# Product keys: gathering the rows of the picked experts instead of streaming all of U and V

## The reference

```python
def _peer(h, w_q, sub_keys, u_tab, v_tab):
    q = (xt @ w_q).reshape(n, PEER_HEADS, 2, PEER_QDIM // 2)
    s = jnp.einsum('nhpd,phkd->nhpk', q, sub_keys).astype(jnp.float32)
    s1, i1 = lax.top_k(s[:, :, 0], K)
    s2, i2 = lax.top_k(s[:, :, 1], K)
    comb = (s1[..., :, None] + s2[..., None, :]).reshape(n, PEER_HEADS, K * K)
    cand = (i1[..., :, None] * PEER_NKEYS + i2[..., None, :]).reshape(n, PEER_HEADS, K * K)
    top_s, pos = lax.top_k(comb, K)
    experts = jnp.take_along_axis(cand, pos, axis=-1)
    gate = jax.nn.softmax(top_s, axis=-1).astype(h.dtype)
    ...
        a = jax.nn.gelu(jnp.einsum('nd,nhkd->nhk', xc, u_tab[ec]))
        return jnp.einsum('nhk,nhkd->nd', gc * a, v_tab[ec])
```

## Time and profile before

| | us |
|---|---|
| median of 3 runs | 2853.23 (2847.7 to 2858.61) |
| span of the profiled execution | 2849.9 |
| TensorE busy | 2686.8 |
| VectorE busy | 1420.1 |
| ScalarE busy | 1154.0 |
| POOL busy | 73.7 |
| DMA moved | 784.12 MB |

### The profile page before, as it was taken

How to read it: one execution, slowest core, us unless ns; L and a number is a source line. 1 busy time by engine, 2 the same in 40 slices (tenths; PEclk the granted TensorE clock), 3 DMA queues, 4 the chain that set the end, 5 groups by cost and what they waited for, 6 DMA issues and landing times.

```text
span 2849.9 us, 53267 instructions
## 1 busy us (share of the span) xinstructions
PE 2686.8 (94%) x20480; PEld 2122.4 (74%) x20480; DVE 1420.1 (50%) x2985; ACT 1154.0 (40%) x2104; POOL 73.7 (3%) x140
## 2 busy tenths in 40 slices
PE   6989989999999999998999999999999999989997
PEld 5769955554545555554878999999998888788997
DVE  2545532222221222222356658887657777656783
ACT  3344321221112211221244454467775544555772
POOL 0000000000000000000000000000000100000000
PEclk9999989999999999999999999999999999999999
DMA  6765689999999989999475556655547777623452
GB/s 246 273 260 220 240 329 422 422 422 422 421 422 423 422 360 422 422 422 393 152 297 203 188 181 222 219 187 168 181 166 251 243 240 241 219 107 131 158 187 104
DMA packets 113215, 784.12 MB, mean 275 GB/s; under 512 B 13488, under 2 KB 13488, under 8 KB 21936
## 3 DMA queue, kind: packets, MB, share of 16 engines
q1 hardware_dynamic: 101808, 741.39, 67.1%
q0 software_dynamic: 11264, 40.71, 4.1%
HBM read 763.96 MB, written 18.09 MB: 274 GB/s over the span
## 4 chain that ended last, share of the span: by engine, by line
PE 78%; DMA 12%; DVE 3%; ACT 3%; SPq 2%; issue 2%; POOL 0%; DVEq 0%; ACTq 0%; POOLq 0%
PE psum L804 15%; PE psum L1451 12%; PE psum L1417 12%; PE psum L1084 11%; DMA weight_ring<-in_stream 9%; PE psum L1116 5%; PE psum L1543 2%; PE psum L671 2%; DMA work<-in_stream 2%; SPq L1599 2%; PE psum L1037 2%; PE psum L1436 2%; PE psum L1046 2%; PE psum L823 1%; PE psum L731 1%
## 5 line engine op out<-in xcount | busy, mean ns | idle before, releaser
L2046 DVE TENSOR_TENSOR work<-psum,work 128x256 f32<-128x256 f32 x132 | 56.1, 425 | 690.6 <-PE psum L1057 690.6
L1678 DVE TENSOR_TENSOR ring_parts<-weight_ring,peer_parts 128x1024 fp32r<-128x1024 f32 x218 | 262.3, 1223 | 252.8 <-ACT peer_parts L2749 208.9
L2749 ACT ACTIVATE peer_parts<-weight_ring 128x1024 fp32r<-128x1024 f32 x218 | 225.0, 1054 | 264.9 <-PE psum L804 118.7
L1116 PE MATMUL psum<-work 128*64 128x512 f32 x1056 | 244.9, 600 | 25.9 <-ACT work L2917 19.3
L1084 PE MATMUL psum<-weight_ring,work 128*64 128x256 f32 x2112 | 244.9, 382 | 16.6 <-DMA weight_ring<-in_stream 15.7
L1451 PE MATMUL psum<-v_high,h_low 128*128 128x512 f32 x1024 | 254.6, 391 | 2.9 <-ACT v_high L3111 2.9
L1084 PEld LDWEIGHTS psum<-weight_ring,work 128*64 128x64 f32 x2112 | 146.5, 137 | 116.0 <-DMA weight_ring<-in_stream 34.1
L1451 PEld LDWEIGHTS psum<-v_high,h_low 128*128 128x128 f32 x1024 | 193.1, 189 | 43.2 <-issue 3.0
L2385 DVE TENSOR_TENSOR ring_parts<-weight_ring,peer_parts 128x1024 fp32r<-128x1024 f32 x128 | 156.8, 1225 | 101.4 <-ACT peer_parts L3067 101.1
L3111 ACT ACTIVATE v_high<-weight_ring 128x1024 fp32r<-128x1024 f32 x128 | 135.8, 1061 | 171.4 <-PE psum L1451 171.4
L2899 ACT ACTIVATE work<-psum 128x256 f32<-128x256 f32 x132 | 50.7, 384 | 363.4 <-PE psum L1084 363.4
(11 more groups left out here) (348 smaller groups left out, 4532.2 us busy)
## 6 DMA issues: line engine op xcount, KB each, us to landing
weight_ring<-in_stream SPq DMA_DIRECT2D x451, 1024.0 KB, 5.3
work<-in_stream SPq DMA_DIRECT2D x192, 1024.0 KB, 23.7
chunkbuf<-in_stream SPq DMA_DIRECT2D x64, 1024.0 KB, 23.6
peer_scores<-chunkbuf POOLq DMA_DIRECT2D x61, 256.0 KB, 5.4
chunkbuf<-peer_scores POOLq DMA_DIRECT2D x61, 256.0 KB, 2.9
work<-in_rows POOLq DMA_DIRECT2D x1, 1312.0 KB, 16.8
xT<-in_x POOLq DMA_DIRECT2D x1, 1024.0 KB, 10.2
work<-in_ctx POOLq DMA_DIRECT2D x1, 1024.0 KB, 18.7
```

The costliest lines, as they stand in the source:

```text
L1116: mm = pe.matmul(psum[h * SEATS:(h + 1) * SEATS, 7, :], m["act_e"][:, 2 * k + f, :], w[:, f, h * 512:(h + 1) * 512], start=(k == 0 and f = ...
L1678: ve.tensor_tensor(split[s].at(ring_parts, q), split[s].at(ring, q), high_halves[:, q % HIGHS, :].bitcast(F32), ALU.subtract).then_inc(spl ...
L2749: sc.activation(high_halves[:, q % HIGHS, :], split[s].at(ring, q), ACT.Copy).then_inc(split[s].high, 1)
```

## The change

The tables U and V lie side by side in one HBM tensor `in_uv` of 16,384 rows of 2048 floats (8 KB), with tokens on the partitions for this layer. A unit is one head of one half of the tokens: 16 units of 16 picks, 256 picks g. For each:

- POOL gathers, for the 128 tokens of its half, the row `expert[token, g]` of `in_uv` into one of 8 places (`EARLY`), 11 from g = 64 on (`LATE` = 3, which lie where the queries and keys were). It waits until the value product of the pick that held the place before is done.
- VectorE multiplies the U half of the row by h (`h_nat`, turned once by TensorE) and sums along the row (`scored`).
- ScalarE takes the gelu of that one number a token, multiplies it by the gate, and writes the identity scaled by it, a diagonal (`diagonal`).
- TensorE multiplies the diagonal by the V half of the row, in plain fp32, 2 x 512 columns, and adds it in PSUM (`values_of`).

The search for unit u+2 stands between the 16 products of unit u on VectorE. The queries and keys of heads 4 to 7 stand between value products on TensorE. `keys` is no longer a piece of the ring but is loaded by POOL. The round trips of x and of the scores, G, the one-hot tables and the 128 streamed pieces are gone, and the result of the first half of the tokens is turned and added to x while the second half is worked on. Weight halves of stage 3 that stood at the layer's end (`highs(0)`, `lows(0)`, `highs(1)`, `lows(1)`) stand between the last picks.

```diff
+EARLY, LATE = 8, 3
+DIAGS = 4
...
-    ("peer_q", 8), ("keys", 1), ("peer", PE_N),
+    ("peer_q", 8),
...
+                def values_of(g):
+                    t = g // (PICKS // TT)
+                    pe.wait_ge(pick_d, g + 1)
+                    for h in range(2):
+                        mm = pe.matmul(psum[:, 2 * t + h, :], m["diag"][:, g % DIAGS, :],
+                                       m["rows_of_uv"][row_place[g]][:, D + h * 512:D + (h + 1) * 512],
+                                       start=(g % (PICKS // TT) == 0), stop=True, skip_group_check=True)
+                    mm.then_inc(pick_v, 1)
...
+                for g in range(PICKS):
+                    if g in (8, 20, 32, 44):
+                        queries(4 + g // 12)
+                    if g in (10, 22, 34, 46):
+                        keyed(4 + g // 12, 5 + 2 * (g // 12 % 2))
...
+                    values_of(g)
...
+                def scored(g):
+                    t, row = g // (PICKS // TT), m["rows_of_uv"][row_place[g]][:, 0:D]
+                    ve.wait_ge(*row_landed(g))
+                    ve.tensor_tensor_reduce(row, row, m["h_nat"][:, t, :], 1.0, 0.0, ALU.mult, ALU.add,
+                                            m["score"][:, g:g + 1]).then_inc(pick_s, 1)
...
+                searched(0, weights_beside)
+                searched(1, lambda k: None)
+                gated(0)
+                gated(1)
...
+                def diagonal(g):
+                    one = slice(g, g + 1)
+                    sc.wait_ge(pick_s, g + 1)
+                    sc.activation(m["gelu"][:, one], m["score"][:, one], ACT.Gelu_apprx_tanh).then_inc(pick_a, 1)
+                    if g % PE_K == 0:
+                        sc.wait_ge(*at(f"gate:{g // PE_K}"))
+                    sc.wait_ge(pick_a, g + 1)
+                    sc.activation(m["weight"][:, one], m["gelu"][:, one], ACT.Copy, scale=m["gate"][:, one]).then_inc(pick_c, 1)
+                    if g >= DIAGS:
+                        sc.wait_ge(pick_v, g - DIAGS + 1)
+                    sc.wait_ge(pick_c, g + 1)
+                    sc.activation(m["diag"][:, g % DIAGS, :], ident[:, :], ACT.Copy, scale=m["weight"][:, one]).then_inc(pick_d, 1)
...
+                for g in range(PICKS):
+                    before = row_before(g)
+                    if g % PE_K == 0:
+                        gp.wait_ge(*at(f"expert:{g // PE_K}"))
+                    if before is not None:
+                        gp.wait_ge(pick_v, before + 1)
...
+                    gp.indirect_dma_start(m["rows_of_uv"][row_place[g]], None, dram["uv"],
+                                          bass.IndirectOffsetOnAxis(ap=m["expert"][:, g:g + 1], axis=0)) \
+                      .then_inc(row_in[row_place[g]], 16)
...
-    u = np.concatenate([u[0::2], u[1::2]], 2)
...
+    W["uv"] = np.concatenate([a["peer_u_2"][0], a["peer_v_2"][0]], 1)
```

More of the change, by code:

```diff
@@ L590, in plan @@
-                m["zs"] = a.take(2, PE_H)
-                m["G"] = work[:, :].rearrange("p (t k) -> p t k", t=T)
-                tables = xT[:, :, :].rearrange("p c t -> p (c t)").rearrange("p (q s k n) -> p q s k n", q=2, s=2, k=CHUNK)
-                last = work[:, 32768 - 2 * CHUNK * PE_N:32768].rearrange("p (q k n) -> p q k n", q=2, k=CHUNK)
-                m["oh1"], m["oh2"] = ([tables[:, q, 0], tables[:, q, 1], last[:, q]] for q in range(2))
-                whole = chunkbuf[:, :, :].rearrange("p a b -> p (a b)")
@@ new lines, in plan @@
+                late = [a.at]
+                m["h_low"] = as_parts(a.take(DC, T), a.at - DC * T)
+                m["sc"] = a.take(TT, 16, PE_N)
+                late.append(a.at)
+                m["pqT"] = a.take(8, T)
+                m["diag"] = a.take(DIAGS, P)
+                m["expert"] = a.take(PICKS).bitcast(U32)
+                m["sums"], m["shares"] = a.take(UNITS), a.take(UNITS)
+                rows_at = 32768 - (EARLY - 1) * SLOT
+                assert a.at <= rows_at
+                late.append(32768 - SLOT)
@@ L2587, in mix3 @@
+                for u in range(UNITS):
+                    unit(u)
+                    if u == PE_H:
+                        residual_of_picks(0, V, mod_cols(2, 5))
+                ve.wait_ge(pick_v, PICKS)
+                ve.tensor_copy(m["y_nat"][:, 1, 512:D], psum[:, 3, :]).then_inc(*V.up("free:y:1:1", "y_nat:1:1"))
+                residual_of_picks(1, V, mod_cols(2, 5))
             def mix3():
@@ L3138, in peer, with exponentials_of_picks @@
[L3138 to L3141 removed]
+                def exponentials_of_picks(u):
+                    sc.wait_ge(*at(f"cand:{u}"))
+                    gate = m["gate"][:, u * PE_K:(u + 1) * PE_K]
+                    act(A_, gate, gate, ACT.Exp, f"cand_exp:{u}", accum_out=m["sums"][:, u:u + 1])
@@ new lines, in peer @@
+                queries(0)
+                queries(1)
+                highs(26, 2)
+                for i in range(4):
+                    sc.wait_ge(*at(f"h_nat:{i}"))
+                    act(A_, m["h_nat"][:, i // 2, (i % 2) * 512:(i % 2 + 1) * 512], bank_of(f"h_nat:{i}"), ACT.Copy,
+                        f"free:h_nat:{i}", *(["h_nat_sb"] if i == 3 else []))
+                scores_of_keys(0)
+                scores_of_keys(1)
+                highs(27, 2)
+                queries(2)
+                scores_of_keys(2)
@@ new lines, in peer @@
+                highs(28, 2)
+                queries(3)
+                scores_of_keys(3)
+                exponentials_of_picks(0)
+                exponentials_of_picks(1)
+                for g in range(PICKS):
+                    diagonal(g)
+                    if g in (9, 21, 33, 45):
+                        queries(4 + g // 12)
+                    if g in (11, 23, 35, 47):
+                        scores_of_keys(4 + g // 12)
+                    if g in (10, 11, 22, 23, 34, 35):
+                        high_half(58 + 2 * (g // 12) + g % 12 - 10, 2)
+                    if g % PE_K == 13 and g // PE_K + 2 < UNITS:
+                        exponentials_of_picks(g // PE_K + 2)
+                    if g == PICKS // TT + 3:
+                        sc.wait_ge(pick_v, PICKS // TT)
+                        for h in range(2):
+                            act(A_, m["y_nat"][:, 0, h * 512:(h + 1) * 512], psum[:, h, :], ACT.Copy, f"free:y:0:{h}",
+                                f"y_nat:0:{h}")
+                    if g in (234, 236, 238, 240):
+                        high_half((g - 234) // 2)
```

608 lines of the change are left out of this document (190 added, 418 removed).

## The result

| | before | changed |
|---|---|---|
| median, us | 2855.92 (2847.7 to 2858.99, 4 runs) | 2696.43 (2693.96 to 2698.39, 4 runs) |
| span of the profiled execution | 2849.9 | 2696.2 |
| TensorE busy | 2686.8 | 2412.8 |
| VectorE busy | 1420.1 | 1243.5 |
| ScalarE busy | 1154.0 | 968.1 |

What follows compares the result with a forecast made beforehand. DMA was taken to bound the changed layer: 1678 + 3 + 666 + 20 + 4 = 2371 against 2488.0, -117, with -5.5 behind it -122.5 from 2853.2, giving 2730 us. Range 2680 to 2900; the forecast's own 2680 to 2780.

Steps and rivals of the forecast that it cites:

- First gather: Start of the edited layer: expert numbers ready and first gather out at 1678, first row scored at 1688.
- Price on VectorE: Per pick, product 1.22 plus sum read 0.13 and a sixteenth of a 10 us search: 1.98, 520 us in all.
- Products in two passes: VectorE's products and sum as two instructions, 2.57 a pick: time 2885; chance 0.11 together with POOL and VectorE taking turns.
- Price on the others: Over the 256 picks: ScalarE 275 us, TensorE 1.72 a pick and under 485 in all, POOL 1.2 a gather, 307.
- the first rival: POOL can't issue gathers fast enough: breaks even at 3.16 us a gather, at 3.6 time 2967; chance 0.19.
- DMA, the term that was mis-sized: Gathered rows: 2.60 us per 1 MB gather, bounds 2.485 and 5.2, 666 us for 256, plus 20 for 8 MB weights.
- End of the values: Last value product of the edited layer ends at 2371, against 2488.0 before: -117.
- Tail: From the last value product to stage 3: a gain of 5.5 us, bounds 0 and 8.
- The loop of the places: Buffer reuse: one round 11 us, over 8 places 1.4 a pick, under 2.60, so bursts elsewhere are covered.
- Random rows slower: 8 KB rows scattered over 128 MB move slower than the stream: time 2837 at 350 GB/s, 2784 at 375; chance 0.13.
- TensorE's clock: Clock falls in TensorE's pauses, at 1.2 GHz 3.5 a pick, time 2950; chance 0.04 together with spread.
- Turns, the rule that was half right: A gather keeps VectorE's product out: at 1.0 us a gather, time 2829; chance 0.11 together with a product in two passes.

Runs made afterwards that it cites:

- the run with half rows: Changed kernel gathering only the 4 KB U row, which also stands in for the V row, all instructions kept: 2512.81 us, ratio 0.8807.
- the plain rows: Changed kernel with each gather replaced by a plain transfer of 128 neighbouring 8 KB rows, same size and place: 2693.64 us, ratio 0.9441.

## Why the prediction was right, and by how much it was off

Its mechanism held: the layer is bound by the bytes of the rows. Each of its steps, with times on the clock of before (the trace of after less the 4.8 us of late arrival):

- **First gather.** Forecast 1678, 33.2 us after the layer's start; it went at 1679.18, 29.6 after it, so 1674.4: 3.6 earlier (2.3 in the profiles in which it goes 30.9 after). The first product was forecast at 1688 and ran at 1688.29, so 1683.5.
- **Price on VectorE.** The product and the read of its sum are 1225 and 82 ns long, against 1.22 + 0.13 forecast, and the read lies within the end of the product (1900.86 in a product from 1899.71 to 1900.94), so that a pick holds VectorE for 1.23. Products in two passes did not come. The search costs less than the 10 us a unit that I put in: of VectorE's 201.34 us in 1850 to 2150 the products take 147.0, which leaves 54.3 for 7.5 units, 7.2 each. The lengths of the search's records add up to 9.5 a unit, as I had added them up, but each begins some 0.08 us before the one ahead of it ends. A sum of mean lengths of short instructions overstates what they cost.

```profile
1899.71 1.23 DVE L2341 CUSTOM_DVE_ANT_0 work<-work 128x1024 f32<-128x1024 f32 x1 [0.77 <-DMA work<-in_uv,work]
1900.86 0.08 DVE L2341 DVE_READ_ACCUMULATOR2_ANT work<- 128x1 f32 x1
...
L2341 DVE CUSTOM_DVE_ANT_0 work<-work 128x1024 f32<-128x1024 f32 x120 | 147.0, 1225 | 99.0 <-DMA work<-in_uv,work 98.9
```

- **Price on the others.** ScalarE: 0.20, 0.295 and, for the diagonal, 0.40, where the earlier trace rows had 0.31 for a 128x128 of another kind. TensorE: 1.70 a pick when it is full (the run with half rows), forecast 1.72. POOL: 1.06 and a pause of 0.30, forecast 1.2, far from the 3.16 of the first rival. None of them sets the pace.
- **DMA, the term that was mis-sized.** I took 2.60 a gather, 3% over the mean of a saturated stretch. It is 2.49, the lower bound: 256 x 0.11 = 28 us. I had reasoned that random rows can't be faster than the stream; they were as fast as its best window, and the plain rows show that the addresses cost nothing. The mean of 414 over 600 us that I started from has its small gaps; in this layer eight or more places leave none. The weights were rightly added, but they are 5.24 MB and not 8, as SP's queue shows for 1679 to 2344:

```profile
q1 hardware_dynamic: 720, 5.24, 1.9%
```

  From the start of the first product (1688.29) to that of the last (2339.22) are 650.9 us for 255 picks, and 255 x 2.49 = 635 leaves 16, where I had 20. In that time 4.19 MB of weights moved, 10 us at 421 GB/s. The rest lies at the end, where the DMA engines do not finish together; two of sixteen would be a share of 0.12:

```profile
2333.00:2338.00 5.00, 4.10 (x9) 1.35 (x8) 2.61 (x6) 1.80 (x6) 0.00 (x0) 1.00 0.11 46
```

  That the 16 comes near my 20 is partly luck.
- **End of the values.** Forecast 2371; 2343.55 less 4.8 is 2338.8: 32 early, 3.6 from the start and 28 from the rate. The 4 less behind the weights and 4 more at the two ends cancel: the first product came 9.1 us after its gather, and I had 3 and a transfer of 2.6.
- **Tail.** From the last value product's end to stage 3 it was 18.1 and is 10.0: -8.1, where I took -5.5 with a bound of -8. The turning starts 0.7 us after the last product (2344.24), where it was 7.1.
- **The sum.** -149.2 (2338.8 against 2488.0), -8.1 and -1.1 behind the layer and +4.8 ahead of it give -153.7, where -122.5 was forecast.
- **The loop of the places.** This step was half right and did no harm. I made a round 11 us and 1.4 a pick with eight places, with about 5.3 for transfer and landing and 4.65 for VectorE, ScalarE and TensorE. Both hold: the engines' part is 4.6, and a lone gather lands in 5.4, counted from its start on POOL, so that most of the 1.2 that I added for POOL is in it already. What I left out is that gathers lengthen each other's landing, to 7.9 with only four places, which makes the round 12.5. With eight places that is 1.56 a pick and stays hidden. But I wrote that without cover "the six columns would cost 35 us", and with four places the whole gain went. The places are worth 150 us, all of it between four and six.
- **The rivals.** POOL: refuted by its 349 us of waiting, though with two gathers a pick it comes close to one. Random rows slower: refuted by 421 GB/s and by the plain rows. TensorE's clock: 0.98 to 1.00 in spite of pauses of 0.5 us in each pick; only the first 30 us of the picks show less, 0.91. Spread over the DMA engines: share 1.01.

**Turns, the rule that was half right.** The prediction left open whether a gather and VectorE's product keep each other out. Timeline of VectorE and POOL, changed kernel:

```profile
2100.47 1.23 DVE L2341 CUSTOM_DVE_ANT_0 work<-work 128x1024 f32<-128x1024 f32 x1 [0.76 <-DMA work<-in_uv,work]
...
2101.57 0.94 POOL L3126 DMA_INDIRECT work<-in_uv,work  x1 [3.02 <-PE psum L1418]
...
2102.96 1.23 DVE L2341 CUSTOM_DVE_ANT_0 work<-work 128x1024 f32<-128x1024 f32 x1 [0.22 <-DMA work<-in_uv,work]
2103.28 1.72 POOL L3126 DMA_INDIRECT work<-in_uv,work  x1 [0.78 <-PE psum L1418]
...
2105.30 0.94 POOL L3126 DMA_INDIRECT work<-in_uv,work  x1 [0.31 <-issue]
```

The gather at 2103.28 starts with 0.91 us of the product left and lasts 1.72 instead of 0.94. Of the 55 gathers that began within a product, 52 follow one rule: such a gather lasts what is left of the product and 0.81 us more, and never under 0.94 (0.36 left gave 1.17, 0.62 gave 1.43, 1.17 gave 1.98). The 164 gathers during whose start VectorE was idle took 0.93 to 0.97, and so did nearly all that met MAX8, FIND_INDEX8 or MATCH_REPLACE8, which read one large tensor. Some that met another operation with two inputs (TENSOR_TENSOR) were drawn out too, up to 1.60. The product itself is 1.23 with and without a gather beside it. So POOL waits for VectorE, and no wait of VectorE for POOL shows: its product takes 1225 ns on average, where the halving of before, with two inputs of the same shape, took 1226 and 1223, and where a gather went out less than 0.8 us ahead of a product (174 times) the product kept its 1.23. As POOL had 349 us to spare, its waits were worth nothing here. The Trainium skill (SBUF — State Buffer, "Who interferes with whom") has the two contend, and one of them wait for the other; for a gather that comes behind the product the trace agrees (1.72 us instead of 0.94), and for the other order it shows no price.

## What to carry to other kernels

When rows are gathered instead of streamed, count the bytes at the DMA rate of a saturated stretch of the same kernel (here 421 GB/s for scattered 8 KB rows too), and put what belongs to one index side by side (here 94 us). Then count the buffers: the lone landing and the engines' part of one round (10.0 us here), over the number of places, has to stay well under the time of one transfer (2.49), not just reach it. Four places reach it and lost 158 us against six; above six more places buy nothing, so the memory can go elsewhere. A reorder at the start of such a stream was worth 2 to 6 us of the layer's length here, less than whole kernels can be told apart by, and how much of the earlier start counts depends on what it delays behind it.

## What the runs showed of the hardware

- A gather of 128 rows of 8 KB costs POOL 0.94 us and a pause of 0.30 to the next, where a plain transfer of the same bytes costs 0.53 (528 ns over 256).
- Scattered rows of 8 KB move as fast as neighbouring ones, 421 GB/s at a DMA share of 1.01. Rows of 4 KB reach 408 to 416 GB/s where gathers are queued; over 300 us they came to 367 at 0.97 with two tables and POOL near its limit, and to 307 at 0.88 with one table and TensorE full.
- A gather of 1 MB that is nearly alone on the DMA engines lands in 5.4 us, the plain 1 MB restore of before took 5.2. With four places the median is 7.9 at a DMA share of 0.91.
- A gather that meets VectorE's product over two tensors is drawn out by what is left of it, up to 1.99 us in all; the plain transfers met the same products and stayed at 0.53.
- VectorE's product with a sum along the row (128x1024, fp32) is two records, 1225 ns and 82 ns, and the second lies within the first.
